# Attention probabilities carry gate over row sum before their transposes, in a two-block float32 layer on one Trainium2 core

## The reference

```python
# fox: c is the running sum of log f; 8 heads, gate silu(g)
s = q . k * D**-0.5 + c[q] - c[k]
o_c = softmax(where(mask, s, -1e30)) @ v
o_c = o_c * silu(g_c)

# NSA: compressed blocks (o_c), selected blocks (o_s), window (o_w); 16 heads in 4 groups
s_s = q . ks - slopes * dist ;  s_w = q . kw - slopes * dist
out = gates[0] * o_c + gates[1] * (p_s @ vs) + gates[2] * (p_w @ vw)
```

## Time and profile before

| what | value |
|---|---|
| median of 3 runs | 1619.98 us (1619.87 to 1620.24) |
| the profiled execution | 1622.98 us, its span 1621.1 us |
| PE, PEld busy | 1565.4 us (97%), 1287.9 us (79%) |
| DVE, ACT, POOL busy | 887.1 us (55%), 700.7 us (43%), 120.5 us (7%) |
| granted clock over the span | 0.991 |
| chain that ended last | PE 77%, DVE 12%, ACT 5%, issue 4% |
| DVE conversion of a weight piece | 1262 ns, x190 |
| DVE conversion of a tile of mix_t to mix_lo | 681 ns, x8 |

### The profile page before, as it was taken

How to read it: one execution, slowest core, us unless ns; L and a number is a source line. 1 busy time by engine, 2 the same in 40 slices (tenths; PEclk the granted TensorE clock), 3 DMA queues, 4 the chain that set the end, 5 groups by cost and what they waited for, 6 DMA issues and landing times.

```text
span 1621.1 us, 34256 instructions
## 1 busy us (share of the span) xinstructions
PE 1565.4 (97%) x14842; PEld 1287.9 (79%) x14842; DVE 887.1 (55%) x1589; ACT 700.7 (43%) x1268; POOL 120.5 (7%) x86
## 2 busy tenths in 40 slices
PE   7999999899999999989999999999999999999998
PEld 6888768789787797888888777888887888888887
DVE  4657363674482654742235787533246677777333
ACT  5543274663432633424235878523225333333222
POOL 0004000002142122421000000000000000000000
PEclk9999999999999999999999999999999999999999
DMA  6322303520010110206322000232342233232232
GB/s 217 105 78 82 127 2 117 185 80 10 28 54 10 53 37 28 54 10 145 78 66 65 2 2 2 66 104 81 102 156 91 79 104 104 79 104 96 74 117 79
DMA packets 110948, 124.44 MB, mean 77 GB/s; under 512 B 21288, under 2 KB 94632, under 8 KB 110416
## 3 DMA queue, kind: packets, MB, share of 16 engines
q1 hardware_dynamic: 107872, 114.85, 22.6%
q10 hardware_dynamic: 2928, 7.41, 1.3%
HBM read 118.04 MB, written 4.21 MB: 75 GB/s over the span
## 4 chain that ended last, share of the span: by engine, by line
PE 77%; DVE 12%; ACT 5%; issue 4%; SPq 1%; DMA 1%; POOL 0%; DVEq 0%; ACTq 0%; POOLq 0%
PE bank L800 73%; PE bank L810 4%; ACT arena L1473 3%; DVE arena L2070 2%; DVE arena L2067 2%; DVE weights_lo L2067 2%; DVE ff_c L2070 1%; ACT L1473 1%; DVE ff_c L2067 1%; DVE act_lo L2067 1%; ACT weights_hi L1473 1%; DVE ff_c L2075 1%; DMA arena<-in_c_rwkv 1%; DVE act_t L2067 1%; DVE arena L2429 0%
## 5 line engine op out<-in xcount | busy, mean ns | idle before, releaser
L1473 ACT ACTIVATE arena<-bank 128x512 f32<-128x512 f32 (+4 forms) x419 | 230.2, 567 | 551.8 <-PE bank L800 519.7
L800 PE MATMUL bank<-h_hi,weights_hi 128*128 128x512 f32 (+1 forms) x1008 | 403.5, 400 | 8.2 <-DVE weights_lo L2067 5.7
L2067 DVE TENSOR_TENSOR weights_lo<-weights,weights_hi 128x1024 fp32r<-128x1024 f32 (+1 forms) x190 | 239.7, 1262 | 303.2 <-ACT weights_hi L1473 296.8
L800 PE MATMUL bank<-h_lo,weights_hi 128*128 128x512 f32 (+1 forms) x1008 | 395.0, 392 | 0.0
L800 PE MATMUL bank<-h_hi,weights_lo 128*128 128x512 f32 (+1 forms) x1008 | 394.7, 392 | 0.0
L800 PE MATMUL bank<-arena 64*64 64x64 f32 (+7 forms) x7746 | 353.7, 248 | 15.5 <-issue 6.9
L800 PEld LDWEIGHTS bank<-arena 64*64 64x64 f32 (+3 forms) x7746 | 281.5, 140 | 64.5 <-issue 55.5
L1473 ACT ACTIVATE weights_hi<-weights 128x1024 fp32r<-128x1024 f32 (+1 forms) x190 | 200.2, 1054 | 168.8 <-PE bank L800 163.8
L800 PEld LDWEIGHTS bank<-h_hi,weights_hi 128*128 128x128 f32 (+1 forms) x1008 | 190.4, 189 | 59.0 <-DVE weights_lo L2067 12.9
L800 PEld LDWEIGHTS bank<-h_hi,weights_lo 128*128 128x128 f32 (+1 forms) x1008 | 190.6, 189 | 40.9
L800 PEld LDWEIGHTS bank<-h_lo,weights_hi 128*128 128x128 f32 (+1 forms) x1008 | 190.9, 189 | 37.5
(11 more groups left out here) (174 smaller groups left out, 1680.5 us busy)
## 6 DMA issues: line engine op xcount, KB each, us to landing
weights<-in_w_in SPq DMA_DIRECT2D x41, 1024.0 KB, 5.4
weights<-in_ffn_up SPq DMA_DIRECT2D x22, 1024.0 KB, 5.1
weights<-in_ffn_down SPq DMA_DIRECT2D x10, 1024.0 KB, 5.1
weights<-in_w_out SPq DMA_DIRECT2D x8, 1024.0 KB, 5.2
weights<-in_w_in SPq DMA_DIRECT2D x16, 256.0 KB, 4.8
weights<-in_w_branch_rwkv SPq DMA_DIRECT2D x4, 1024.0 KB, 5.3
weights<-in_w_branch_nsa SPq DMA_DIRECT2D x4, 1024.0 KB, 5.2
arena<-in_x SPq DMA_DIRECT2D x4, 512.0 KB, 6.4
```

The source lines that it names most:

```text
L800: return pe.matmul(o, w, x, start=first, stop=last)
L1473: return act.activation(o, i, f, **kw)
L2067: return dve.tensor_tensor(o, a, b, op)
```

## The change

The factors are applied on DVE, to the probability tiles themselves and before they are transposed: `scale(k)` waits for the four exponentials of quad k, makes the factors, and multiplies each tile in place by its column. PE's products that spread the factors are gone. In NSA both branches add up in the same 128 columns of one bank, so `nsa_finish` is one sum; `fox_finish` is one product. The step order is new on all three engines: on PE S(s) whole, V(s-3), T(s-2) whole; on ACT exp(s) whole and one step earlier, then the copies of T(s-2); on DVE all minima of s, finish(s-3), scale(s-1).

```diff
@@ PE @@
                 def turn(k, n):
-                    pe.wait_ge(sem("probs_ready"), 4 * (done + k) + units[-1] + 1)
+                    pe.wait_ge(sem("probs_scaled"), 4 * (done + k) + units[-1] + 1)
...
+                def values(k):
+                    j = order["V", k]
+                    for b in range(2):
+                        for n in turn_jobs(k, b):
+                            wait_read(pe, order["T", k, n])
+                    claim(pe, j)
+                    units = quad(k)
+                    one = name == "nsa"
+                    for b in range(2):
+                        at_ = 0 if one else b * P
+                        for n in range(tile_of(k) + 1):
+                            for x in range(2):
+                                ins = mm(ps(j)[x * DH:x * DH + DH, at_:at_ + P], units[2 * b + x][2][n],
+                                         pt[:, (4 * k + 2 * b + x) % 8, n * P:(n + 1) * P],
+                                         n == 0 and not (one and b), n == tile_of(k) and not (one and b == 0))
+                    fill(j, ins)
                 for s in range(quads + 3):
-                    for b in range(2):
-                        if s < quads:
+                    if s < quads:
+                        for b in range(2):
                             scores(s, b)
-                        if 0 <= s - 2 < quads:
+                    if s >= 3:
+                        values(s - 3)
+                    if 0 <= s - 2 < quads:
+                        for b in range(2):
                             for n in turn_jobs(s - 2, b):
                                 turn(s - 2, n)
...
-                        pe.wait_ge(sem("factors_ready"), done + k + 1)
-                        for b in range(2):
-                            for x in range(2):
-                                ins = mm(ps(j)[x * DH:x * DH + DH, 256 + b * P:256 + (b + 1) * P],
-                                         across(factors(k)[:, 2 * b + x:2 * b + x + 1]), ident)
-                        fill(j, ins)
@@ ACT @@
-                    for b in range(2):
-                        if 0 <= s - 1 < quads:
-                            for x in range(2):
-                                exponential(s - 1, 2 * b + x)
-                        if s >= 2:
+                    if s < quads:
+                        for n in range(4):
+                            exponential(s, n)
+                    if s >= 2:
+                        for b in range(2):
                             for n in turn_jobs(s - 2, b):
                                 copy_turned(s - 2, n)
@@ DVE @@
-                for s in range(quads + 4):
+                def scale(k):
+                    dve.wait_ge(sem("probs_ready"), 4 * (done + k + 1))
+                    then(factor(k))
+                    for n in range(4):
+                        prob = unit(probs, 4 * k + n)[:, 0:(tile_of(k) + 1) * P]
+                        ts(prob, prob, factors(k)[:, n:n + 1]).then_inc(sem("probs_scaled"), 1)
+
+                for s in range(quads + 3):
                     if s < quads:
-                        for n in range(2):
+                        for n in range(4):
                             minimum(s, n)
-                    if s >= 4:
-                        wait_full(dve, order["V", s - 4])
-                        finish(s - 4, order["V", s - 4])
-                    if s < quads:
-                        for n in range(2, 4):
-                            minimum(s, n)
-                    if 0 <= s - 2 < quads:
-                        dve.wait_ge(sem("probs_ready"), 4 * (done + s - 1))
-                        factor(s - 2).then_inc(sem("factors_ready"), 1)
+                    if s >= 3:
+                        wait_full(dve, order["V", s - 3])
+                        finish(s - 3, order["V", s - 3])
+                    if 0 <= s - 1 < quads:
+                        scale(s - 1)
@@ fox_finish @@
-                two = ps(j).rearrange("p (m b t) -> p m b t", m=2, b=2)
-                m = mark(tt(o, two[:, 0], silu_gc[:, tiles, tok], ALU.mult))
-                after(m)
-                read(j, tt(o, two[:, 1], o, ALU.mult))
+                read(j, tt(o, ps(j)[:, 0:256].rearrange("p (b t) -> p b t", b=2), silu_gc[:, tiles, tok], ALU.mult))
@@ nsa_finish @@
-                two = ps(j).rearrange("p (m b t) -> p m b t", m=2, b=2)
-                then(dve.tensor_copy(nsa_two, two[:, 1]))
-                read(j, tt(nsa_two, two[:, 0], nsa_two, ALU.mult))
-                wait_read(dve, j)
-                for b in range(2):
-                    then(tt(o, o, nsa_two[:, b, :], ALU.add))
+                read(j, tt(o, o, ps(j)[:, 0:P], ALU.add))
```

More of the change, by code:

```diff
@@ L921, in attend @@
                                 turn(s - 2, n)
-                    if s >= 3:
-                        k = s - 3
-                        j = order["V", k]
-                        for b in range(2):
[L926 to L929, removed]
-                        for b in range(2):
-                            for n in range(tile_of(k) + 1):
-                                for x in range(2):
-                                    ins = mm(ps(j)[x * DH:x * DH + DH, b * P:(b + 1) * P], units[2 * b + x][2][n],
-                                             pt[:, (4 * k + 2 * b + x) % 8, n * P:(n + 1) * P], n == 0, n == tile_of(k))
-                        pe.wait_ge(sem("factors_ready"), done + k + 1)
-                        for b in range(2):
-                            for x in range(2):
-                                ins = mm(ps(j)[x * DH:x * DH + DH, 256 + b * P:256 + (b + 1) * P],
-                                         across(factors(k)[:, 2 * b + x:2 * b + x + 1]), ident)
-                        fill(j, ins)
```

4 lines of the change are left out of this document (1 added, 3 removed).

## The result

The changed kernel takes 1649.2 us in the median of four runs (1644.1 to 1650.9), the one before 1619.9 (1619.5 to 1620.2). The ratio is 1.0176, with a 95% interval from 1.0153 to 1.0199: 29.3 us slower, where 13.2 was forecast, and outside the range given. The profiled execution of the changed kernel is its fastest, 1644.1 us, with a span of 1642.3; the span of the one before is 1621.1. So the two traces differ by 21.2 us, and not by 29.3.

The account below looks back on a forecast made before the run. TensorE bounds the kernel now; after the change a ring of waits would. NSA 7.2 (3.6 + 2.4 + 1.2) plus fox 6.0 gives 13.2 us slower: 1636.2 profiled, 1633.2 median, range 1618 to 1641.

Parts of the forecast that it names:

- What bounds the kernel: NSA phase: TensorE is busy in 144.00 of 144 us and is the whole chain of waits.
- the order costs more than it saves: Both attention phases: engines wait in a ring, using up TensorE's gain; 13.2 us slower in all.
- The parts: Per NSA head: TensorE's work falls from 18.0 to 15.2 us; VectorE's four scalings at width 4 take 1.62 us.
- the rival of one element per cycle: VectorE scaling: width 4 about 0.27 us longer each, 1.06 per head, giving 1644 us; chance 0.10.
- The ring: NSA, one V4 to the next: waits through TensorE, ScalarE and VectorE sum to 18.2 us a head; chance 0.70.
- The hops: Handovers between engines in the ring, such as 0.06 us from ScalarE's copies to TensorE and 0.04 from minimum to ScalarE.
- V4: TensorE's values of a quad with four key tiles, where the ring is counted from; taken as 1.79 us.
- The start of NSA: NSA's first V4 comes 3.6 us later, as VectorE first makes factors and scaling of quads 0 and 1.
- Fox: The other attention phase, eight quads: start 3.4, stretch to second V4 1.4, end 1.2; 6.0 us slower.
- The end of NSA: From NSA's last V4 to the merge: 8.2 us against 7.0, so 1.2 slower, as TensorE waits for the copies.
- The seven heads: NSA up to the last V4: 7 x 18.2 = 127.3 us against 124.9, 2.4 slower.
- the second stretch: From the y1 projection behind fox to NSA's first scores, instructions the same in both kernels: forecast change 0.

Follow-up runs that it names:

- Order alone: Changed kernel's step order, but factors spread by TensorE and applied in the finish as in the kernel before: 1644.9 us, 1.0141 against the kernel before.
- the repeat: The changed kernel run once more, unedited: 1649.6 us, 1.0176 against the kernel before.
- the run with scaling first: Changed kernel with VectorE's scaling of quad s-1 ahead of the finish of quad s-3: 1635.1 us, 1.0090 against the kernel before.
- without scaling: Changed kernel with the multiplication of probabilities by factors left out, factors still made and semaphore kept: 1629.2 us, 1.0048 against the kernel before.
- With the wait filled: Changed kernel plus 8 unused identity products on TensorE before its wait for copies in width-4 NSA quads, values' bank claimed earlier: 1636.4 us, 1.0113 against the kernel before.

## Why the prediction was wrong

- *What bounds the kernel, and that the order costs more than it saves:* right. Order alone is 1.4% slower, the same work with a step more between copies and values is 0.85% faster than before.
- *The parts:* PE's work of 15.2 us per head is right to the row (15.20), the scalings are 482, 415, 348 and 282 ns (485, 418, 352, 285), so the rival of one element per cycle fell. Four of width 4 took 1.67 us (1.62), not 1.94: the section of the Trainium skill that the prediction sets against its rows ("VectorE: DVE Perf Modes", The DRAIN you can't avoid) says itself that a next instruction that is not held starts earlier, and the prediction left that out.
- *The ring:* right in each of its links, 18.67 instead of 18.2. The hops were too small: from the end of ACT's last copy to PE it is about 0.25 us, not 0.06 (1.85 and 2.27 for copies with hop, 1.70 and 2.17 forecast), V4 is 1.90 up to the transposes (1.79), the two hops from minimum to exponential 0.12 more together. I took the hop to PE from a timeline in which PE waited for nothing. 0.47 us a head is 3.3 in seven.
- *The start of NSA:* 15.69 us from scores to the first V4 against 12.01, 3.7 (3.6). *Fox:* V4 at 228.26 and 248.47, forecast 228.2 and 248.3; with the end +6.8 (6.0). In this profile that is partly luck: the stage began 1.6 us earlier than before the change, and the granted clock of 211 to 222 us was 0.84. In the repeat, with neither (0.98), V4 was at 228.16, so the links are right; there the second V4 took 3.21 us behind a wait of 2.65, and fox was +8.4.
- *The end of NSA:* 10.47 us against 7.0, 3.5 (1.2). 1.6 of it is clock (V4 3.33 and its transposes 1.34), the rest hops: the run with scaling first has 8.85 where nothing was slow, and 8.2 was forecast.
- *The seven heads,* forecast +2.4, are +12.1: 3.3 more by the ring, and 6.4 by the clock, in four heads (9.6 in six, in the repeat). **This is the step that failed:** the prediction said "PE then idles for 3.0 us of each head" (measured 3.47) and priced this idleness at itself. It had a second price: in most heads what came behind the wait ran at the lower clock, 1.6 us a head, and here it is the longest PE piece of the ring. With it the sum is 13.2 + 3.9 (ring 3.3, hops at the end 0.6) + 8.0 to 11.2 (clock in heads and end), 25 to 28; with the second stretch left out, the two traces are 26.0 and 29.8 us above before, and fox has the rest.
- *The range* ended at 1641, since nothing in it stood for the clock. The kernel before gave no clear warning. In fox, with its wait of 1.73 us, the granted clock of 205 to 250 us was 0.96, where NSA without waits had 1.00; but it was low ahead of that wait (0.63 from 204.1 to 208.7 us) and 1.00 behind it (211 to 222).

## What to carry to other kernels

Before steps are moved closer together, follow the dependences once around the loop and add the hop wherever an engine will really have to wait (here 0.25 us from ACT to PE and 0.1 from DVE to ACT); shares of busy time say nothing about this. If a link is taken out, look for the path that is just behind it: twice here (0.78 instead of 1.6 us, 0.16 instead of 1.0) it was within a microsecond. A wait that a change puts into TensorE's queue costs itself and, where the granted clock falls behind it, more (here 1.6 us behind one of 2.4); one more step of distance, where buffers allow, removed both in NSA here; fox was 3.5 us longer with it until VectorE's order was changed too.

## What the runs showed of the hardware

- The granted clock fell behind a wait, in the midst of a busy phase. Before V4 in NSA, behind 2.36 to 2.37 us: 10 of 12 times. Behind 1.59 to 1.65 us (without scaling, order alone, scaling first): 0 of 18. With the wait filled, 0.28 us left: 0 of 6. Before the last V4, where the wait was longest: behind 2.25 us once of twice (without scaling, scaling first), behind 2.63 to 3.02 us 3 of 3.
- The length of one wait does not decide it alone. In fox the spreading of factors took 1.97 us behind 2.74 us (the repeat) and 3.63 us behind 1.74 (the run without scaling); 16 transposes ran at 0.52 behind 1.10 us; and two waits of under 1 us were enough for one head of seven. What else decides, these runs don't settle.
- The Trainium skill, "TensorE: Matmul & The Clock Gate", HAM oscillation — how this bites in real kernels, describes a kernel that waits for a transfer in every round of its loop and starts each round at the lower clock, and advises an order in which the engine stays busy. The traces agree, with a wait for ScalarE in place of the transfer: 0.55 in the window of V4, a slow V4 round after round in the repeat, and 1.00 once the wait was filled.
- A wait that is already met still takes its place in PE's queue: with the claim of the bank behind the wait for the copies instead of ahead of it, PE started the values about 0.1 us later (1.85 and 2.27 us behind the first copy instead of 1.73 and 2.17). That the claim was met by then is read from the order of the banks, not from a trace.
